# Prompt retention with masked scores of all chunks at once instead of a state carried from chunk to chunk

## The chip, the cores and the metric

One core of one Trainium2 chip. The metric is the device time of one execution in microseconds, the median of several runs; lower is better. All data are fp32; the large projections are computed with operands split into a high and a low part.

## What is computed

The program is one inference step of a decoder with two layers: layer 0 is differential attention, layer 1 multi-scale retention. Both serve a prompt of 512 tokens and eight samples of 8 tokens. The change concerns the retention of the prompt, for each of 8 heads with 256 key and 512 value dimensions. The reference, cut to it:

```python
RET_CHUNK = 128
def retention_chunk(s_prev, q, k, v, log_g):
    c = q.shape[2]
    idx = jnp.arange(c, dtype=jnp.float32)
    diff = idx[:, None] - idx[None, :]
    decay = jnp.where(diff >= 0, jnp.exp(log_g[:, None, None] * jnp.maximum(diff, 0.0)), 0.0)
    scores = jnp.einsum('bhid,bhjd->bhij', q, k) * decay
    o = (jnp.einsum('bhij,bhje->bhie', scores, v)
         + jnp.einsum('bhid,bhde->bhie', q, s_prev) * jnp.exp(log_g[:, None] * (idx + 1.0))[:, :, None])
    k_dec = k * jnp.exp(log_g[:, None] * (c - 1.0 - idx))[:, :, None]
    s_new = jnp.exp(log_g * c)[:, None, None] * s_prev + jnp.einsum('bhjd,bhje->bhde', k_dec, v)
    return s_new, o
```

`retention_prompt` scans this over the four chunks of the prompt from a state of zeros. The outputs `o` are normalised per head, multiplied by the silu of the gate and go through the output projection; the last state is an output too.

## The kernel before, in words

The order of the work is written out by hand as one list of stages, which every engine walks for its own part; semaphores between them carry counts. In layer one a head takes 192 slots. Each slot holds one projection tile (L923): six matmuls of 288 moving columns (high x high, high x low, low x high, each on two halves of the 576 tokens). Eight tiles use one chunk of weights: ScalarE copies it to WH (L1170), VectorE forms the rest WL (L1438), and the first tile of the next chunk waits for it; the tiles of slots that are multiples of 8 open a chunk. Two banks of PSUM are switched every four tiles; at the end of each 32 tiles ScalarE evacuates them (L1186, slots 156 and 159, 188 and 191 among others), and PE needs them free at the next multiple of 32. Between the tiles `retention_work` (L427) puts the retention of the head whose projection is under way:

- slot 100: load of the head's table `hc` (L881), 389 columns of masks and decays, on SyncE's queue; then loads of the sample states and of weights on the same queue
- slot 136: `rs_keys` (PE L1047, ScalarE L1309, VectorE L1634), scores and keys of the samples; VectorE also forms the decayed queries `qd` (L1638) and `qz`
- slot 138: `pad_rows` (L1314), ScalarE issues eight small DMAs that spread the samples' rows, once the keys are copied
- slots 139 + 12c: `ret_scores` (PE L1058): two matmuls of 128 columns (keys of chunk c against queries of chunk c) into bank 4, and two transposes of the keys into bank 5. VectorE masks bank 4 into `sT` (L1664, L1667), ScalarE copies bank 5, scaled, into `kd` (L1324)
- slots 144 + 12c: `ret_out` (L1069): one matmul `sT` x values, and for c > 0 two more, decayed queries x state, 512 columns each, into bank 6; ScalarE copies and squares the result (L1328)
- slots 146 + 12c: `ret_state` (L1079): two matmuls `kd` x values, 512 columns, into banks 4 and 5; VectorE takes them over into the state `Sp` (L1669; a copy for c = 0, L1676 with the decay for c > 0)
- slot 152: `rs_mask` (L1653) for the samples; slot 187: store of the state; slots 190 to 226: norm, gate and store; from 228: the samples' outputs and states, which reach into the slots of the next head.

Each PE stage waits for the banks it writes to be drained (`free`). In the trace all matmuls carry the line of the helper `mm` (L918), all transposes that of `tr` (L921), the copies of ScalarE L1160. An fp32 matmul has two records.

Of the kernel before, what the change touches and what calls it, by code (L numbers as in the profile page):

```python
# [24 lines left out]
MASKED = -1e30  # L25
HC = 128 + 128 + 64 + 64 + 2 + 1 + 2
KRING, VRING = 4, 8
# [7 lines left out]
def shape_tables():  # L35
# [28 lines left out]
    for h in range(HEADS):  # L64
        lg = math.log1p(-2.0 ** (-5 - h))
        w = 1.0 / 16
        diff = i[None] - i[:, None]
        dec = np.where(diff >= 0, np.exp(lg * np.maximum(diff, 0)), 0) * w
        t = row % NQ
        ds = t[None] - t[:, None]  # L70
        decs = np.where((ds >= 0) & (row[None] // NQ == row[:, None] // NQ), np.exp(lg * np.maximum(ds, 0)), 0) * w
        pad = lambda a: np.concatenate([a, np.zeros((128 - a.shape[0], a.shape[1]))])
        spread = lambda a: np.broadcast_to(a[None], (128, a.size))
        r = np.arange(128)
        kz = np.where((r % 32 < 2 * NQ)[:, None] & ((r % 32 // NQ)[:, None] == np.arange(2)[None]),
                      np.exp(lg * (NQ - 1.0 - r % NQ))[:, None], 0) * w
        heads.append(np.concatenate([dec, spread(np.exp(lg * (i + 1))), spread(np.exp(lg * (t + 1.0))), pad(decs), pad(kz),
                                     (np.exp(lg * (127.0 - i)) * w)[:, None],
                                     spread(np.exp(lg * np.array([128.0, 8.0])))], 1))
    eye = np.concatenate([np.eye(128), np.ones((128, 128))], 1)  # L80
# [346 lines left out]
def retention_work(h):  # L427
# [3 lines left out]
    def put(t, *s):  # L431
        at.setdefault(t, []).extend(s)
# [12 lines left out]
    for c in range(4):  # L445
        put(139 + 12 * c, Stage("ret_scores", c=c))
        put(144 + 12 * c, Stage("ret_out", c=c))
        put(146 + 12 * c, Stage("ret_state", c=c))
    put(187, Stage("store_state_p"))
# [181 lines left out]
def hybrid_step_kernel(nc, x_prompt, x_sample, cache_k, cache_v, page_table, state_ret, norm_pre_attn, w_in_attn,  # L631
# [30 lines left out]
    with ctx:  # L662
# [58 lines left out]
        rvT, rqT, rkT = lay("rvT", [128, 2, T]), lay("rqT", [128, 2, T]), lay("rkT", [128, 2, T])  # L721
        qd, kd, Sp = lay("qd", [128, 2, SEQ]), lay("kd", [128, 256]), lay("Sp", [128, 2, 512])
        assert used[0] == KT * T
        hc, rvn, rsg, oN = lay("hc", [128, HC]), lay("rvn", [128, 5, 512]), lay("rsg", [128, 4, T]), lay("oN", [128, 5, 512])
        Sin, sT = lay("Sin", [128, NB, 1024]), lay("sT", [128, 128])
        sTz, qz = lay("sTz", [SMP, 128]), lay("qz", [128, 2, 2, 128])
# [182 lines left out]
        def _(pe):  # L909
# [148 lines left out]
            def ret_scores(g, c_):  # L1058
                lo = c_ * 128
                free(4)  # L1060
                for e in range(2):
                    last = mm(bank[4][:, 0:128], rkT[:, e, lo:lo + 128], rqT[:, e, lo:lo + 128], start=e == 0, stop=e == 1)
                last.then_inc(sem["full4"], 1)
                free(5)
                for e in range(2):
                    last = tr(bank[5][:, e * 128:(e + 1) * 128], rkT[:, e, lo:lo + 128])
                last.then_inc(sem["full5"], 1)

            def ret_out(g, c_):  # L1069
                for n in ("drained4", "drained5", "qd_ready", "drained7"):  # L1070
                    pe.wait_ge(sem[n], c.before(n))
                free(6)
                last = mm(bank[6][:, :], sT[:], rvn[:, c_, :], start=True, stop=c_ == 0)
                if c_:
                    for e in range(2):
                        last = mm(bank[6][:, :], qd[:, e, c_ * 128:c_ * 128 + 128], Sp[:, e, :], start=False, stop=e == 1)
                last.then_inc(sem["full6"], 1)

            def ret_state(g, c_):  # L1079
                free(4)  # L1080
                free(5)
                for e in range(2):
                    mm(bank[4 + e][:, :], kd[:, e * 128:(e + 1) * 128], rvn[:, c_, :]).then_inc(sem[f"full{4 + e}"], 1)

# [49 lines left out]
            def x_tr(g, t, in_low, after, freed):  # L1134
# [7 lines left out]
                for b in range(4):  # L1142
                    for j in range(4):
# [6 lines left out]
                                  rs_keys=rs_keys, ret_scores=lambda g, c: ret_scores(g, c), ret_out=lambda g, c: ret_out(g, c),  # L1150
                                  ret_state=lambda g, c: ret_state(g, c),
                                  rs_state=rs_state, rs_out=rs_out, gate=gate, y_rstd=y_rstd, y_tr=y_tr, x_tr=x_tr))
# [3 lines left out]
        def _(act):  # L1156
# [167 lines left out]
            def ret_scores(g, c_):  # L1324
                act.wait_ge(sem["full5"], c.done("full5"))
                copy(kd[:], bank[5][:, 0:256], scale=hc[:, 386:387]).then_inc(sem["drained5"], 1)

# [79 lines left out]
        def _(dve):  # L1407
# [226 lines left out]
            def rs_keys(g):  # L1634
                dve.wait_ge(sem["head_in"], c.before("head_in"))
                for n in ("full6", "rotated"):
                    dve.wait_ge(sem[n], c.before(n))
                o.link(v.tensor_tensor(qd[:].rearrange("p e (c i) -> p e c i", c=4), rqT[:, :, 0:SEQ].rearrange("p e (c i) -> p e c i", c=4),  # L1638
                                       hc[:, 128:256].rearrange("p (e c i) -> p e c i", e=1, c=1).broadcast_to([128, 2, 4, 128]), MUL))
                for b_ in range(2):  # L1640
                    mine = lambda a: a.rearrange("p e (j b i) -> p e j b i", b=2, i=NQ)[:, :, :, b_, :]
                    ins = v.tensor_tensor(qz[:, b_, :, :].rearrange("p e (j r) -> p e j r", r=32)[:, :, :, b_ * NQ:(b_ + 1) * NQ],
                                          mine(rqT[:, :, SEQ:T]),
                                          mine(hc[:, 256:320].rearrange("p (e n) -> p e n", e=1)).broadcast_to([128, 2, 4, NQ]), MUL)
                    if b_:
                        ins.then_inc(sem["qd_ready"], 1)
                    else:
                        o.link(ins)
                dve.wait_ge(sem["full4"], c.done("full4"))
                v.tensor_tensor(sTz[:].rearrange("p (j r) -> p j r", r=32)[:, :, 0:16], bank[4][0:SMP, 0:SMP].rearrange("p (j r) -> p j r", r=16),  # L1650
                                hc[0:SMP, 320:384].rearrange("p (j r) -> p j r", r=16), MUL).then_inc(sem["drained4"], 1)

            def rs_mask(g):  # L1653
# [3 lines left out]
                for b_ in range(2):  # L1657
                    ins = v.tensor_scalar(kz[:, b_, :], knz[:], hc[:, 384 + b_:385 + b_], None, MUL)
                    if b_:
                        ins.then_inc(sem["kz_ready"], 1)  # L1660
                    else:
                        o.link(ins)

            def ret_scores(g, c_):  # L1664
                dve.wait_ge(sem["full6"], c.before("full6"))
                dve.wait_ge(sem["full4"], c.done("full4"))
                v.tensor_tensor(sT[:], bank[4][:, 0:128], hc[:, 0:128], MUL).then_inc(sem["drained4"], 1)  # L1667

            def ret_state(g, c_):  # L1669
                dve.wait_ge(sem["full6"], c.before("full6"))  # L1670
                dve.wait_ge(sem["sp_out"], c.before("sp_out"))
                for e in range(2):
                    dve.wait_ge(sem[f"drained{4 + e}"], c.before(f"drained{4 + e}"))
                    dve.wait_ge(sem[f"full{4 + e}"], c.done(f"full{4 + e}"))
                    if c_:
                        ins = v.scalar_tensor_tensor(out=Sp[:, e, :], in0=Sp[:, e, :], scalar=hc[:, 387:388], in1=bank[4 + e][:, :],  # L1676
                                                     op0=MUL, op1=ADD)
                    else:
                        ins = v.tensor_copy(Sp[:, e, :], bank[4 + e][:, :])
                    ins.then_inc(sem[f"drained{4 + e}"], 1)  # L1680

# [8 lines left out]
            def rs_state(g, g_, e):  # L1690
                dve.wait_ge(sem["full6"], c.before("full6"))
                for j in range(4):
                    dve.wait_ge(sem[f"full{4 + j}"], c.done(f"full{4 + j}"))
                    mine = Sin[:, 2 * j + g_, e * 512:(e + 1) * 512]
                    v.scalar_tensor_tensor(out=mine, in0=mine, scalar=hc[:, 388:389], in1=bank[4 + j][:, :], op0=MUL, op1=ADD  # L1695
                                           ).then_inc(sem[f"drained{4 + j}"], 1)
# [58 lines left out]
            def x_tr(g, t, in_low, after, freed):  # L1755
                R, src = TILES[t][1], (high, low)[in_low]
                for b in range(4):
# [9 lines left out]
                                sample_gate=sample_gate, carry=carry, rope=rope_, load_rope=load_rope,  # L1767
                                ret_scores=lambda g, c: ret_scores(g, c), ret_state=lambda g, c: ret_state(g, c),
                                ret_norm=ret_norm, ret_rstd=ret_rstd, rs_keys=rs_keys, rs_mask=rs_mask, rs_state=rs_state, gate=gate))


# [72 lines left out]
```

## Time and profile before

| what | value |
|---|---|
| median of 3 runs | 3944.06 us (3943.42 to 3957.97) |
| the profiled execution: its time | 3945.5 us |
| its span, first to last instruction | 3943.7 us |
| mean granted TensorE clock | 0.985 of full |
| the eight heads' retention | from about 2050 to 3460 us of the span |

The page's busy time counts each engine by itself; the list of waits gives, for one engine, how long it sat idle and what released it. A timeline row is one group of equal instructions in a row: start, length, engine, line, operation, output from inputs, number of records, and in brackets the idle time before it. The end of a matmul is modelled and holds the drain of the array, so rows of PE overlap.

### The profile page before, as it was taken

The page shows a single profiled execution, that of the slowest core. Times are in us where ns is not written, and L with a number is a line of the kernel's source. Part 1 is how long each engine was busy: PE and PEld are TensorE (multiplying, and loading weights), DVE is VectorE, ACT ScalarE, POOL GpSimd, SP SyncE. Part 2 cuts the span into 40 slices and gives each one's busy share as a digit, 9 for nine tenths or more (in the row PEclk, how much of TensorE's full clock was granted, in tenths as well). Part 3 has the DMA queues.
Part 4 walks back from the last instruction along what each step waited for, and adds up shares of the span by engine and source line. Part 5 has one row for each costly group of instructions (what it writes and reads, how often), then busy time and mean ns, then how long its engine had stood idle before and what let it go on. Part 6 is the DMA issues. An engine that isn't in the chain of part 4 may idle for free.

```text
span 3943.7 us, 70016 instructions
## 1 busy us (share of the span) xinstructions
PE 3741.5 (95%) x27060; PEld 3298.5 (84%) x27060; DVE 1438.5 (36%) x2197; ACT 1101.9 (28%) x1776; POOL 149.3 (4%) x75
## 2 busy tenths in 40 slices
PE   7999999999999997999899999999999999989998
PEld 6987787778777876777898888988898988879998
DVE  3243334433443344334623333333242424233344
ACT  4233233323332333221422222222222222222221
POOL 1000000200020002002200000000000000000000
PEclk9999999999999998999999999999999999989999
DMA  4455777777767776764332424242434343343332
GB/s 146 143 178 178 235 231 233 209 236 231 236 205 236 231 235 188 234 201 167 122 119 84 161 82 154 82 156 89 151 103 133 109 133 120 121 141 120 105 123 97
DMA packets 470428, 636.62 MB, mean 161 GB/s; under 512 B 39569, under 2 KB 293138, under 8 KB 466962
## 3 DMA queue, kind: packets, MB, share of 16 engines
q1 hardware_dynamic: 405762, 559.90, 45.8%
q10 hardware_dynamic: 64336, 72.24, 5.3%
q8 instruction: 217, 3.56, 0.4%
q14 instruction: 113, 0.93, 0.1%
HBM read 559.80 MB, written 70.65 MB: 160 GB/s over the span
## 4 chain that ended last, share of the span: by engine, by line
PE 80%; DVE 4%; ACT 2%; DMA 2%; issue 2%; ACTq 2%; SPq 1%; POOL 1%; DVEq 0%
PE low_banks L918 58%; PE high_banks L918 15%; PE high_banks L921 8%; DVE WL L1440 1%; DMA area<-in_cache_k 1%; ACT WH L1160 1%; DVE area L1695 1%; ACTq L1352 1%; POOL area L1782 1%; SPq L853 1%; ACTq L1321 1%; ACTq L1322 1%; DMA area<-in_cache_v 0%; ACT area L1160 0%; SPq L854 0%
## 5 line engine op out<-in xcount | busy, mean ns | idle before, releaser
L918 PE MATMUL low_banks<-XH,WH 128*128 128x288 f32 x6656 | 1521.7, 309 | 52.2 <-DVE WL L1440 23.4
L918 PE MATMUL low_banks<-XH,WL 128*128 128x288 f32 x6656 | 1443.4, 297 | 0.0
L918 PE MATMUL low_banks<-XL,WH 128*128 128x288 f32 x6656 | 1441.6, 297 | 0.0
L918 PEld LDWEIGHTS low_banks<-XH,WH 128*128 128x128 f32 x6656 | 1078.0, 191 | 146.8 <-issue 95.8
L918 PEld LDWEIGHTS low_banks<-XL,WH 128*128 128x128 f32 x6656 | 1083.9, 190 | 0.0
L918 PEld LDWEIGHTS low_banks<-XH,WL 128*128 128x128 f32 x6656 | 1082.1, 190 | 0.0
L1440 DVE TENSOR_TENSOR WL<-WR,WH 128x1024 fp32r<-128x1024 f32 x424 | 518.9, 1224 | 902.0 <-ACT WH L1160 896.2
L1160 ACT ACTIVATE WH<-WR 128x1024 fp32r<-128x1024 f32 x424 | 448.6, 1058 | 973.1 <-PE low_banks L918 660.1
L918 PE MATMUL high_banks<-area 128*32 128x512 f32 (+6 forms) x3760 | 658.8, 543 | 51.1 <-DVE area L1667 13.0
L1160 ACT ACTIVATE area<-high_banks 128x512 f32<-128x512 f32 x480 | 270.6, 568 | 1187.4 <-PE high_banks L921 833.2
L921 PEld LDWEIGHTS high_banks<-eye_sb,area 128*128 128x128 f32 (+2 forms) x3032 | 347.9, 142 | 199.6 <-issue 132.5
L921 PE MATMUL high_banks<-eye_sb,area 128*128 128x128 f32 (+2 forms) x3032 | 433.8, 279 | 79.2 <-DVE area L1752 19.5
L918 PEld LDWEIGHTS high_banks<-area 128*32 128x32 f32 (+2 forms) x3760 | 249.1, 148 | 277.1 <-issue 217.2
L1523 DVE COPY area<-high_banks 128x512 f32<-128x512 f32 x256 | 177.1, 692 | 544.1 <-PE high_banks L921 480.9
L1782 POOL TENSOR_TENSOR area<-area,power 128x1 f32<-128x1 f32 (+3 forms) x66 | 124.7, 1890 | 3768.5 <-DVE area L1412 3292.2
L1219 ACT ACTIVATE area<-low_banks 128x288 f32<-128x288 f32 x192 | 78.8, 411 | 355.9 <-PE low_banks L918 339.5
L1695 DVE SCALAR_TENSOR_TENSOR area<-area,high_banks 128x512 f32<-128x512 f32 x128 | 87.2, 745 | 50.6 <-PE high_banks L918 50.4
L1676 DVE SCALAR_TENSOR_TENSOR area<-area,high_banks 128x512 f32<-128x512 f32 x48 | 35.9, 747 | 165.8 <-PE high_banks L918 163.8
L1458 DVE TENSOR_TENSOR area<-low_banks,area 128x288 f32<-128x288 f32 x80 | 36.6, 458 | 140.0 <-PE low_banks L918 139.7
L1220 ACT ACTIVATE area<-low_banks 128x288 f32<-128x288 f32 x192 | 79.0, 411 | 6.1
L1708 DVE TENSOR_TENSOR area<-high_banks,area 128x512 f32<-128x512 f32 (+1 forms) x40 | 25.6, 641 | 113.6 <-PE high_banks L921 113.6
L1445 DVE TENSOR_TENSOR XL<-XL,XH 128x576 fp32r<-128x576 f32 (+1 forms) x48 | 36.1, 752 | 45.4 <-ACT XH L1160 44.1
(106 smaller groups left out, 910.7 us busy)
## 6 DMA issues: line engine op xcount, KB each, us to landing
area<-in_cache_k SPq DMA_DIRECT2D x512, 256.0 KB, 4.1
area<-in_cache_v SPq DMA_DIRECT2D x512, 256.0 KB, 3.9
WR<-in_w_in_ret SPq DMA_DIRECT2D x196, 512.0 KB, 3.6
WR<-in_w_in_attn SPq DMA_DIRECT2D x132, 512.0 KB, 5.4
out<-area ACTq DMA_DIRECT2D x73, 512.0 KB, 4.5
area<-in_state_ret SPq DMA_DIRECT2D x64, 512.0 KB, 5.6
WR<-in_w_out_ret SPq DMA_DIRECT2D x64, 512.0 KB, 3.3
WR<-in_w_out_attn SPq DMA_DIRECT2D x32, 512.0 KB, 5.4
```

The source lines that it names most:

```text
L853: page = sp.value_load(pt[0:1, b * PAGES + p:b * PAGES + p + 1], min_val=0, max_val=src.shape[0] - 1)
L918: return nc.tensor.matmul(out, a, b, start=start, stop=stop, skip_group_check=True)
L921: return nc.tensor.matmul(out, a, ident[0:n, 0:n], start=True, stop=True, is_transpose=True, skip_group_check=True)
L1160: return nc.scalar.activation(out, in_, ACT.Copy, scale=scale)
L1219: o.link(nc.scalar.activation(dst[:, 0:HALF], bank[2 * cb][:, 0:HALF], f))
L1220: last = nc.scalar.activation(dst[:, HALF:T], bank[2 * cb + 1][:, 0:HALF], f)
L1321: act.dma_start(knz[padded, :], kn_s[rows, :]).then_inc(sem["padded_in"], 16)
L1322: act.dma_start(rvz[padded, :], rvn[rows, 4, :]).then_inc(sem["padded_in"], 16)
L1440: v.tensor_tensor(WL[:, slot, :, :], WR[:, slot, :, :], WH[:, slot, :, :].bitcast(f32), SUB).then_inc(sem["w_lo"], 1)
L1523: v.tensor_copy(KTs[u % 2][:, :, pp * 128:(pp + 1) * 128], bank[5][:, :].rearrange("p (j s) -> p j s", j=4)).then_inc(sem["drained5"], 1)
L1695: v.scalar_tensor_tensor(out=mine, in0=mine, scalar=hc[:, 388:389], in1=bank[4 + j][:, :], op0=MUL, op1=ADD).then_inc(sem[f"drained{4 + j} ...
L1782: nc.gpsimd.tensor_tensor(out, a, power[0:R, 0:n], ALU.pow).then_inc(sem[name], 1)
```

## The change

The state isn't carried between chunks. Chunk c's keys are multiplied with the queries of chunks c to 3 (512 - 128c columns), masked with a decay table of 512 columns and kept in four buffers; the output of chunk c is the sum over k = 0 .. c of scores times values, in PSUM. The decayed keys of all four chunks are kept, scaled with one column each for the distance to the end of the prompt, and the state is formed once, by four accumulated matmuls for each half. The decayed queries go. The stages move: `ret_scores` to 139 + 5c, `ret_out` to 148 + 8c, `ret_state` to 177, once. The table has 647 columns.

```diff
-HC = 128 + 128 + 64 + 64 + 2 + 1 + 2
+DEC_S, MASK_S, ROWS_S, DEC_K, DEC_8, HC = 512, 576, 640, 642, 646, 647
...
-        diff = i[None] - i[:, None]
+        diff = np.arange(512.0)[None] - i[:, None]
...
     for c in range(4):
-        put(139 + 12 * c, Stage("ret_scores", c=c))
-        put(144 + 12 * c, Stage("ret_out", c=c))
-        put(146 + 12 * c, Stage("ret_state", c=c))
+        put(139 + 5 * c, Stage("ret_scores", c=c))
+        put(148 + 8 * c, Stage("ret_out", c=c))
+    put(177, Stage("ret_state"))
...
-        qd, kd, Sp = lay("qd", [128, 2, SEQ]), lay("kd", [128, 256]), lay("Sp", [128, 2, 512])
+        kd, Sp = lay("kd", [128, 4, 256]), lay("Sp", [128, 2, 512])
...
-        Sin, sT = lay("Sin", [128, NB, 1024]), lay("sT", [128, 128])
+        Sin = lay("Sin", [128, NB, 1024])
+        sT = [lay(f"sT{c}", [128, SEQ - 128 * c]) for c in range(4)]
...
                 for e in range(2):
-                    last = mm(bank[4][:, 0:128], rkT[:, e, lo:lo + 128], rqT[:, e, lo:lo + 128], start=e == 0, stop=e == 1)
+                    last = mm(bank[4][:, 0:SEQ - lo], rkT[:, e, lo:lo + 128], rqT[:, e, lo:SEQ], start=e == 0, stop=e == 1)
...
             def ret_out(g, c_):
-                for n in ("drained4", "drained5", "qd_ready", "drained7"):
+                for n in ("drained4", "drained7"):
                     pe.wait_ge(sem[n], c.before(n))
                 free(6)
-                last = mm(bank[6][:, :], sT[:], rvn[:, c_, :], start=True, stop=c_ == 0)
-                if c_:
-                    for e in range(2):
-                        last = mm(bank[6][:, :], qd[:, e, c_ * 128:c_ * 128 + 128], Sp[:, e, :], start=False, stop=e == 1)
+                for k in range(c_ + 1):
+                    last = mm(bank[6][:, :], sT[k][:, (c_ - k) * 128:(c_ - k + 1) * 128], rvn[:, k, :], start=k == 0, stop=k == c_)
...
-            def ret_state(g, c_):
+            def ret_state(g):
                 free(4)
                 free(5)
                 for e in range(2):
-                    mm(bank[4 + e][:, :], kd[:, e * 128:(e + 1) * 128], rvn[:, c_, :]).then_inc(sem[f"full{4 + e}"], 1)
+                    for k in range(4):
+                        last = mm(bank[4 + e][:, :], kd[:, k, e * 128:(e + 1) * 128], rvn[:, k, :], start=k == 0, stop=k == 3)
+                    last.then_inc(sem[f"full{4 + e}"], 1)
...
-                copy(kd[:], bank[5][:, 0:256], scale=hc[:, 386:387]).then_inc(sem["drained5"], 1)
+                copy(kd[:, c_, :], bank[5][:, 0:256], scale=hc[:, DEC_K + c_:DEC_K + c_ + 1]).then_inc(sem["drained5"], 1)
...
-                o.link(v.tensor_tensor(qd[:].rearrange("p e (c i) -> p e c i", c=4), rqT[:, :, 0:SEQ].rearrange("p e (c i) -> p e c i", c=4),
-                                       hc[:, 128:256].rearrange("p (e c i) -> p e c i", e=1, c=1).broadcast_to([128, 2, 4, 128]), MUL))
...
                 dve.wait_ge(sem["full4"], c.done("full4"))
-                v.tensor_tensor(sT[:], bank[4][:, 0:128], hc[:, 0:128], MUL).then_inc(sem["drained4"], 1)
-
-            def ret_state(g, c_):
-                dve.wait_ge(sem["full6"], c.before("full6"))
+                n = SEQ - 128 * c_
+                v.tensor_tensor(sT[c_][:], bank[4][:, 0:n], hc[:, 0:n], MUL).then_inc(sem["drained4"], 1)
+
+            def ret_state(g):
                 dve.wait_ge(sem["sp_out"], c.before("sp_out"))
                 for e in range(2):
-                    dve.wait_ge(sem[f"drained{4 + e}"], c.before(f"drained{4 + e}"))
                     dve.wait_ge(sem[f"full{4 + e}"], c.done(f"full{4 + e}"))
-                    if c_:
-                        ins = v.scalar_tensor_tensor(out=Sp[:, e, :], in0=Sp[:, e, :], scalar=hc[:, 387:388], in1=bank[4 + e][:, :],
-                                                     op0=MUL, op1=ADD)
-                    else:
-                        ins = v.tensor_copy(Sp[:, e, :], bank[4 + e][:, :])
-                    ins.then_inc(sem[f"drained{4 + e}"], 1)
+                    v.tensor_copy(Sp[:, e, :], bank[4 + e][:, :]).then_inc(sem[f"drained{4 + e}"], 1)
```

## Rows read from the trace of the kernel before

**Rows 1.** The page, busy time of PE: share of the span, instructions.
```profile
PE 3741.5 (95%) x27060; PEld 3298.5 (84%) x27060; DVE 1438.5 (36%) x2197; ACT 1101.9 (28%) x1776; POOL 149.3 (4%) x75
```

**Rows 2.** PE's waits from 2050 to 3460 us: releaser, total, times, longest (all of them).
```profile
PE low_banks L918 <- DVE WL L1440: 13.7, 7, 2.0
PE high_banks L918 <- DVE area L1667: 13.0, 8, 2.2
```

**Rows 3.** Timeline of PE in head 1, the retention of the prompt.
```profile
2246.08 0.61 PE L918 MATMUL high_banks<-area 128*128 128x128 f32 x4
...
2252.14 1.13 PE L918 MATMUL high_banks<-area 128*128 128x512 f32 x2 [1.25 <-DVE area L1667]
...
2260.39 0.61 PE L918 MATMUL high_banks<-area 128*128 128x128 f32 x4
...
2265.04 2.74 PE L918 MATMUL high_banks<-area 128*128 128x512 f32 x6
...
2269.21 1.88 PE L918 MATMUL high_banks<-area 128*128 128x512 f32 x4
...
2274.92 0.61 PE L918 MATMUL high_banks<-area 128*128 128x128 f32 x4
```

**Rows 4.** Timeline of ACT and its queue in head 1.
```profile
2243.90 0.38 ACT L1160 ACTIVATE area<-high_banks 64x256 f32<-64x256 f32 x1 [1.92 <-PE high_banks L921]
2244.31 0.54 ACTq L1321 DMA_DIRECT2D area<-area  x1
...
2248.72 0.61 ACTq L1322 DMA_DIRECT2D area<-area  x1
2249.44 1.06 ACT L1160 ACTIVATE WH<-WR 128x1024 fp32r<-128x1024 f32 x1 [5.16 <-issue]
...
2267.86 0.60 ACT L1160 ACTIVATE area<-high_banks 128x512 f32<-128x512 f32 x1 [4.70 <-PE high_banks L918]
...
2269.26 0.41 ACT L1219 ACTIVATE area<-low_banks 128x288 f32<-128x288 f32 x1
```

**Rows 5.** Timeline of DVE in head 1.
```profile
2250.53 1.23 DVE L1440 TENSOR_TENSOR WL<-WR,WH 128x1024 fp32r<-128x1024 f32 x1 [6.75 <-ACT WH L1160]
2251.79 0.29 DVE L1667 TENSOR_TENSOR area<-high_banks,area 128x128 f32<-128x128 f32 x1
```

**Rows 6.** DVE's groups by shape, 2050 to 3460 us: count, busy us, mean ns, idle before.
```profile
L1676 DVE SCALAR_TENSOR_TENSOR area<-area,high_banks 128x512 f32<-128x512 f32 x48 | 35.9, 747 | 165.8 <-PE high_banks L918 163.8
L1708 DVE TENSOR_TENSOR area<-high_banks,area 128x512 f32<-128x512 f32 x28 | 19.4, 695 | 69.2 <-PE high_banks L921 69.2
...
L1667 DVE TENSOR_TENSOR area<-high_banks,area 128x128 f32<-128x128 f32 x32 | 9.4, 293 | 42.4 <-PE high_banks L918 41.8
```

**Rows 7.** Timeline of PE around the same wait in heads 0, 2, 4 and 6.
```profile
2060.49 1.84 PE L918 MATMUL high_banks<-area 128*128 128x512 f32 x2 [2.09 <-DVE area L1667]
...
2070.35 0.61 PE L918 MATMUL high_banks<-area 128*128 128x128 f32 x4
...
2443.13 2.07 PE L918 MATMUL high_banks<-area 128*128 128x512 f32 x2 [2.19 <-DVE area L1667]
...
2828.17 1.13 PE L918 MATMUL high_banks<-area 128*128 128x512 f32 x2 [1.50 <-DVE area L1667]
...
3210.61 1.66 PE L918 MATMUL high_banks<-area 128*128 128x512 f32 x2 [2.05 <-DVE area L1667]
```

**Rows 8.** Stretches with PE alone: us, busy (records), granted clock, DMA share, GB/s.
```profile
2060.80:2064.10 3.30, 3.30 (x11) 0.50 0.49 159
...
2443.10:2446.40 3.30, 3.27 (x8) 0.50 0.52 159
...
3211.10:3214.40 3.30, 3.30 (x12) 0.50 0.51 159
...
2826.00:2833.00 7.00, 5.50 (x29) 1.00 0.26 80
```

**Rows 9.** The page's DMA issues: count, KB each, us from issue to landing.
```profile
area<-ret_heads SPq DMA_DIRECT2D x8, 194.5 KB, 3.5
```

More of the change, by code:

```diff
@@ L76, in shape_tables @@
                       np.exp(lg * (NQ - 1.0 - r % NQ))[:, None], 0) * w
-        heads.append(np.concatenate([dec, spread(np.exp(lg * (i + 1))), spread(np.exp(lg * (t + 1.0))), pad(decs), pad(kz),
-                                     (np.exp(lg * (127.0 - i)) * w)[:, None],
-                                     spread(np.exp(lg * np.array([128.0, 8.0])))], 1))
+        heads.append(np.concatenate([dec, spread(np.exp(lg * (t + 1.0))), pad(decs), pad(kz),
+                                     np.exp(lg * (511.0 - i[:, None] - 128 * np.arange(4)[None])) * w,
+                                     spread(np.exp(lg * np.array([8.0])))], 1))
     eye = np.concatenate([np.eye(128), np.ones((128, 128))], 1)
@@ L721, in hybrid_step_kernel @@
         rvT, rqT, rkT = lay("rvT", [128, 2, T]), lay("rqT", [128, 2, T]), lay("rkT", [128, 2, T])
-        qd, kd, Sp = lay("qd", [128, 2, SEQ]), lay("kd", [128, 256]), lay("Sp", [128, 2, 512])
-        assert used[0] == KT * T
+        kd, Sp = lay("kd", [128, 4, 256]), lay("Sp", [128, 2, 512])
+        assert used[0] <= KT * T
+        used[0] = KT * T
         hc, rvn, rsg, oN = lay("hc", [128, HC]), lay("rvn", [128, 5, 512]), lay("rsg", [128, 4, T]), lay("oN", [128, 5, 512])
-        Sin, sT = lay("Sin", [128, NB, 1024]), lay("sT", [128, 128])
+        Sin = lay("Sin", [128, NB, 1024])
+        sT = [lay(f"sT{c}", [128, SEQ - 128 * c]) for c in range(4)]
         sTz, qz = lay("sTz", [SMP, 128]), lay("qz", [128, 2, 2, 128])
@@ L1150, in _ @@
                                   rs_keys=rs_keys, ret_scores=lambda g, c: ret_scores(g, c), ret_out=lambda g, c: ret_out(g, c),
-                                  ret_state=lambda g, c: ret_state(g, c),
+                                  ret_state=ret_state,
                                   rs_state=rs_state, rs_out=rs_out, gate=gate, y_rstd=y_rstd, y_tr=y_tr, x_tr=x_tr))
@@ L1643, in rs_keys @@
                                           mine(rqT[:, :, SEQ:T]),
-                                          mine(hc[:, 256:320].rearrange("p (e n) -> p e n", e=1)).broadcast_to([128, 2, 4, NQ]), MUL)
+                                          mine(hc[:, DEC_S:DEC_S + SMP].rearrange("p (e n) -> p e n", e=1)).broadcast_to([128, 2, 4, NQ]), MUL)
                     if b_:
@@ L1650, in rs_keys @@
                 v.tensor_tensor(sTz[:].rearrange("p (j r) -> p j r", r=32)[:, :, 0:16], bank[4][0:SMP, 0:SMP].rearrange("p (j r) -> p j r", r=16),
-                                hc[0:SMP, 320:384].rearrange("p (j r) -> p j r", r=16), MUL).then_inc(sem["drained4"], 1)
+                                hc[0:SMP, MASK_S:MASK_S + SMP].rearrange("p (j r) -> p j r", r=16), MUL).then_inc(sem["drained4"], 1)
             def rs_mask(g):
@@ L1657, in rs_mask @@
                 for b_ in range(2):
-                    ins = v.tensor_scalar(kz[:, b_, :], knz[:], hc[:, 384 + b_:385 + b_], None, MUL)
+                    ins = v.tensor_scalar(kz[:, b_, :], knz[:], hc[:, ROWS_S + b_:ROWS_S + b_ + 1], None, MUL)
                     if b_:
@@ L1694, in rs_state @@
                     mine = Sin[:, 2 * j + g_, e * 512:(e + 1) * 512]
-                    v.scalar_tensor_tensor(out=mine, in0=mine, scalar=hc[:, 388:389], in1=bank[4 + j][:, :], op0=MUL, op1=ADD
+                    v.scalar_tensor_tensor(out=mine, in0=mine, scalar=hc[:, DEC_8:DEC_8 + 1], in1=bank[4 + j][:, :], op0=MUL, op1=ADD
                                            ).then_inc(sem[f"drained{4 + j}"], 1)
@@ L1767, in _ @@
                                 sample_gate=sample_gate, carry=carry, rope=rope_, load_rope=load_rope,
-                                ret_scores=lambda g, c: ret_scores(g, c), ret_state=lambda g, c: ret_state(g, c),
+                                ret_scores=lambda g, c: ret_scores(g, c), ret_state=ret_state,
                                 ret_norm=ret_norm, ret_rstd=ret_rstd, rs_keys=rs_keys, rs_mask=rs_mask, rs_state=rs_state, gate=gate))
```

## The prediction, made before the changed kernel was run

> **What bounds the kernel now.** I read the page's busy line first: TensorE (PE) is busy 3741.5 us of a span of 3943.7 [rows 1]. Its work is therefore the time, and only two things can shorten the kernel: less PE work, or less idle time of PE. VectorE at 36% and ScalarE at 28% cost something only where PE waits for them, so instructions saved there are worth nothing by themselves.
>
> Next comes the list of PE's waits in the stretch of layer one that holds the eight heads [rows 2]. It has two entries alone: 13.0 us in 8 waits for L1667, the VectorE mask of the scores, and 13.7 us in 7 waits for the low half of a weight chunk (WL). There is no wait for L1676, the update of the running state. The chain from chunk to chunk that the change does away with costs PE nothing today.
>
> The timeline of PE in head 1 says the same [rows 3]. From the second score block at 2260.39 to the third at 2274.92 lie 14.53 us. They hold 12 projection tiles, one score block (about 0.6) and five matmuls of 512 columns. One of these is 2.74 - 1.88 = 0.86 us (six records against four, two records to a matmul), so 4.3 in all, and 9.6 us stay for 12 tiles, 0.80 each. The sum closes with no gap. The only gap of this stretch is the 1.25 us ahead of 2252.14, the first output matmul of the head, at slot 144.
>
> Where does that gap come from? On ScalarE [rows 4] the copy at 2243.90 is followed by eight DMA issues for the padded rows, from 2244.31 to 2249.33. Only behind them runs the split of the weights into WH (2249.44, 1.06 us). VectorE takes its turn for WL at 2250.53 and for the first mask at 2251.79 [rows 5]. PE starts at 2252.14, 0.06 us behind the mask's end. This chain starts from rs_keys (slot 136), ahead of the first score block: it doesn't know how long that block is. This is what the forecast hangs on.
>
> **The change, part by part.** *PE, scores.* Chunk c's score matmuls get 512 - 128c moving columns in place of 128, two matmuls each. Extra columns in a head: 2 x (384 + 256 + 128) = 1536. Price: two matmuls of 512 columns show 1.88 us, two of 128 show 0.61 [rows 3]; the drain at the end is the same in both, so 1.27 us for 768 columns, 1.65 ns a column. That is 2.54 us a head, **+20.3 us** for eight. No engine hides it, since PE itself is the bound.
>
> *PE, outputs and state.* Before: 1 + 3 + 3 + 3 = 10 matmuls of 512 columns for the outputs; after: 1 + 2 + 3 + 4 = 10. State: 4 x 2 before, 2 x 4 after. Transposes of the keys: 8 and 8. All of this at **0**. Accumulating in PSUM moves the additions from VectorE into matmuls that were there already.
>
> *VectorE.* It loses the decayed queries (L1638) and six state updates of 0.747 us a head, two copies out of PSUM stay; its masks grow from 4 x 0.293 to something between 0.293 and 0.695 each (L1708 is the same kind of operation on 128x512 out of PSUM) [rows 6]. PE doesn't wait for these operations but at the first mask, so they count 0 on the path, and that one mask counts +0.40 us. ScalarE keeps all its copies, with another scale column: 0.
>
> *The wait at slot 144.* The first output matmul moves to slot 148, and the second score block comes to slot 144 in its place. It needs bank 4 free, hence the same first mask. So the wait changes its owner, and isn't removed by the move. But in head 1 PE would come to slot 144 1.27 us later, at 2250.89 + 1.27 = 2252.16; the mask would end at 2251.79 + 0.695 = 2252.49, and with 0.06 us for the release PE goes on at 2252.55, after 0.39 us. Over the heads the mean wait is 13.0 / 8 = 1.63; new 1.63 - 1.27 + 0.40 = 0.76, in sum 6.1, so **-6.9 us**. Bounds: all of it gone (-13.0), or nothing absorbed and the mask longer (+3.2).
>
> *The clock.* After three of the eight waits, those of 2.09, 2.19 and 2.05 us, PE's granted clock was 0.50 (1.2 GHz) for a stretch; after the wait of 1.50 it stayed at 1.00, 2.4 GHz [rows 7, 8]. Price: from the first output matmul to the second score block head 0 took 2070.35 - 2060.49 = 9.86 us, head 1 2260.39 - 2252.14 = 8.25 for the same work [rows 3, 7], so 1.61 us for a fall. The longest of these waits would shrink to 2.19 - 0.87 = 1.32, below the 1.50 that did no harm. I take all three falls as gone: **-4.8 us**. Bounds: none gone (0), or a fall in all eight heads (+8.1).
>
> Here the Trainium skill speaks otherwise: its page "TensorE: Matmul & The Clock Gate", section "HAM oscillation — how this bites in real kernels", counts only idle gaps longer than any of these as a cause of a throttled clock. By it the three falls would have another cause and would stay, and the sum would lack the 4.8 us. The trace has the fall right behind each of the three longest waits, so my sum goes by the rows.
>
> *What else moves.* The second to fourth score blocks each wait for the mask before them; they stand 5 tiles (4 us) apart, and the masks take 0.7 at most. At slot 156 the output block is followed by the evacuation of the projection's banks, which PE needs at slot 160. ScalarE takes 2269.26 - 2267.86 = 1.40 us for its two passes over the output [rows 4] and 0.82 for the evacuation's two copies of 0.41. Today 1.7 us of state matmuls stand in between as well; afterwards only 4 tiles, 3.2 us, cover 0.06 + 1.40 + 0.82 = 2.3. It holds with 0.9 us over: 0. The state's 8 matmuls become one block of 6.9 us at slot 177; VectorE then splits the next WL behind its two copies, and PE wants that only 7 tiles (5.6 us) after the block: 0. The head table grows from 389 to 647 columns, so its load from 194.5 KB to 323.5; it takes 3.5 us now [rows 9] and is issued at slot 100 for use at 136, 29 us later: 0 even at twice the time. The 13.7 us of waits for WL come from slots that the change doesn't touch, behind DMA issues for the sample states: 0, with some luck in whether a clock fall follows them.
>
> **Sum:** +20.3 - 6.9 - 4.8 = +8.6 us. Against the profiled execution's own span that is 3943.7 + 8.6 = 3952.3. Its time was 3945.5, which is 1.8 above the span and 1.4 above the median of the three runs (3944.06). Carried to the median: 3952.7.
>
> **The rivals.** (1) *The clock's falls stay.* They follow from something else than the waits' length, or the shorter waits do it too. For it: the waits for WL, of up to 2.0 us [rows 2], are followed by a fall in three of seven cases by my count, so the length alone does not decide. Sum +20.3 - 6.9 = +13.4, so 3957.5. The skill's rule ends here too.
>
> (2) *The wait isn't absorbed; slower.* Place: slot 144. If ScalarE's DMA issues and its split of WH come later by what PE loses in the longer block, PE waits the full 1.63 and the longer mask: 16.2 us in all, +3.2, with a mean of 2.03 us. That is the length at which the clock fell [rows 7, 8], so it would fall in all eight heads, five more: +8.1. Sum 20.3 + 3.2 + 8.1 = +31.6, so 3975.7. It decides, with the falls as they are today, from the point where less than 3.8 of the 16.2 us is absorbed (20.3 + 3.2 - 3.8 = 19.7); with more falls earlier. Against it: the chain starts from a copy ahead of the score block [rows 4]; for it: the wait was 1.25 us in one head and 2.19 in another, so this chain is not a fixed one [rows 3, 7].
>
> (3) *More comes back.* The emptier VectorE and the longer block leave no wait at slot 144 (-13.0), no fall there (-4.8), and the falls behind the WL waits, I count three, don't come by luck (-4.8): 20.3 - 22.6 = -2.3, so 3941.8.
>
> (4) *Faster by more than can be told.* All waits and falls of these heads together, 13.0 + 13.7 + 4.8 + 4.8 = 36.3, against 20.3 would give -16.0, 3928.1. Even this isn't outside the 0.5%, so only something that no row shows could do it.
>
> **How the numbers follow.** A measurement of this kernel can tell about 0.5% from no change, 19.7 us. Forecast 0.54; rival (1) 0.22; rival (2) 0.10; rival (3) 0.12; rival (4) 0.02. The forecast, (1) and (3) lie within 0.5%: same 0.88; slower 0.10 from (2), faster 0.02 from (4). The range takes in (3) at its low end and (1) with a few falls of the clock on top, each 1.6 us: 3941 to 3963. Left out are (2), (4) and a little at both ends.
>
> **What would show it.** In the profile after: PE's busy time up by some 20 us; two score matmuls of 512 columns at 1.88 us; no state updates (L1676) on VectorE any more; in the list of PE's waits the mask stays the releaser, now of a score block, with about 6 us in 8 waits of at most 1.4; the same 13.7 us for WL; the clock at 1.00 behind every score block. A mask wait of over 1.5 us, or one at a place other than slot 144, would make me wrong, and a total beyond 3963.8 us would mean that the longer blocks opened a wait which I have costed at nothing.

## The result and the profile after

The changed kernel takes **3960.26 us** (median of 19 runs, 3956.92 to 3967.49), the kernel before 3945.91 (19 runs, 3937.18 to 3957.97) measured along with it. The ratio is 1.0039, 95% interval 1.0033 to 1.0045. That is slower by 0.4%, some 14 to 15 us, and inside the 0.5% that the prediction called "same". The forecast was +8.6. The direction holds; some 40% of the size is missing from the forecast and has to be found. Two runs taken later, one of the changed kernel at 5893.86 us (mean granted clock 0.582) and one of the kernel before at 5256.97 (0.652), ran at a far lower clock and are left out of the ratios and medians below.

The profiled execution took 3957.83 us, with a span of 3956.0. Its busy line, which answers to [rows 1]:

```profile
PE 3757.1 (95%) x27060; PEld 3302.8 (83%) x27060; DVE 1398.8 (35%) x2141; ACT 1102.2 (28%) x1776; POOL 149.4 (4%) x75
```

VectorE lost 39.7 us of work and 56 instructions, ScalarE nothing, and PE gained 15.6 us of busy time with the same number of records where the prediction named some 20 (busy time falls where the clock is higher, and this profile has three falls of the clock fewer in the retention, so this isn't the price of the columns by itself). Line numbers have moved by one or two: mm is L920, tr L923, ScalarE's copies L1162, the mask L1668, WL L1442.

PE's waits between 2050 and 3475 us, all of them, against [rows 2] (who waited, releaser, total, times, longest):

```profile
PE low_banks L920 <- DVE WL L1442: 13.7, 7, 2.0
PE high_banks L920 <- DVE area L1668: 4.6, 8, 1.1
PE low_banks L920 <- ACT area L1222: 0.6, 1, 0.6
```

The 13.0 us behind the first mask have become 4.6. The waits for WL are the same to a tenth. A third entry is new, of one wait.

Timeline of PE in head 1, against [rows 3]:

```profile
2250.05 1.88 PE L920 MATMUL high_banks<-area 128*128 128x512 f32 x4
...
2256.51 1.56 PE L920 MATMUL high_banks<-area 128*128 128x384 f32 x4 [0.36 <-DVE area L1668]
...
2262.96 1.03 PE L920 MATMUL high_banks<-area 128*128 128x256 f32 x4
...
2268.04 0.61 PE L920 MATMUL high_banks<-area 128*128 128x128 f32 x4
...
2278.38 2.74 PE L920 MATMUL high_banks<-area 128*128 128x512 f32 x6
...
2287.35 3.60 PE L920 MATMUL high_banks<-area 128*128 128x512 f32 x8
...
2294.77 7.04 PE L920 MATMUL high_banks<-area 128*128 128x512 f32 x16
```

The score blocks shrink from 1.88 to 0.61 us, the output blocks grow by one matmul each, and the state is one block of eight matmuls. The wait stands ahead of the second score block, at slot 144, with 0.36 us where the prediction worked out 0.39 for this very head.

Timeline of DVE in head 1, against [rows 5]:

```profile
2254.50 1.22 DVE L1442 TENSOR_TENSOR WL<-WR,WH 128x1024 fp32r<-128x1024 f32 x1 [6.76 <-ACT WH L1162]
2255.76 0.69 DVE L1668 TENSOR_TENSOR area<-high_banks,area 128x512 f32<-128x512 f32 x1
```

Behind the late WL comes the wide mask with 0.69 us. So far the profile agrees with the steps. What remains is the clock. Stretches of PE (us, busy and records, granted clock, DMA share, GB/s): three behind waits for WL and one behind the wait at slot 144.

```profile
2206.10:2209.40 3.30, 3.30 (x16) 0.50 0.88 273
2591.90:2595.20 3.30, 3.30 (x16) 0.50 0.93 304
2977.60:2980.90 3.30, 3.30 (x16) 0.50 0.89 286
...
2256.00:2262.00 6.00, 5.64 (x35) 1.00 0.28 90
```

Behind none of the eight waits for the mask does the clock fall to 1.2 GHz any more. It falls behind three of the seven waits for WL, in every second head. In the kernel before it was three falls behind the mask and three behind WL.

### The profile page after: what moved, and what is told of

Same layout as the page of the kernel before. It is cut to its first block and busy times, and to the rows that moved or that the text cites. A ratio compares the mean times of both kernels' runs of the same rounds, so it can differ in the third digit from the quotient of the medians.

```text
span 3956.0 us, 69816 instructions
## 1 busy us (share of the span) xinstructions
PE 3757.1 (95%) x27060; PEld 3302.8 (83%) x27060; DVE 1398.8 (35%) x2141; ACT 1102.2 (28%) x1776; POOL 149.4 (4%) x75
## 5 line engine op out<-in xcount | busy, mean ns | idle before, releaser
L920 PE MATMUL low_banks<-XH,WH 128*128 128x288 f32 x6656 | 1510.3, 307 | 53.8 <-DVE WL L1442 22.3
L920 PE MATMUL low_banks<-XH,WL 128*128 128x288 f32 x6656 | 1444.3, 297 | 0.0
L920 PE MATMUL low_banks<-XL,WH 128*128 128x288 f32 x6656 | 1442.8, 297 | 0.0
L920 PEld LDWEIGHTS low_banks<-XH,WH 128*128 128x128 f32 x6656 | 1077.1, 191 | 135.6 <-issue 85.3
L920 PEld LDWEIGHTS low_banks<-XH,WL 128*128 128x128 f32 x6656 | 1083.8, 190 | 0.0
L920 PEld LDWEIGHTS low_banks<-XL,WH 128*128 128x128 f32 x6656 | 1082.7, 190 | 0.0
L1442 DVE TENSOR_TENSOR WL<-WR,WH 128x1024 fp32r<-128x1024 f32 x424 | 519.0, 1224 | 1002.0 <-ACT WH L1162 996.3
L1162 ACT ACTIVATE WH<-WR 128x1024 fp32r<-128x1024 f32 x424 | 448.5, 1058 | 1065.1 <-PE low_banks L920 752.0
L920 PE MATMUL high_banks<-area 128*32 128x512 f32 (+6 forms) x3760 | 672.6, 548 | 43.5 <-DVE area L1525 11.3
L1162 ACT ACTIVATE area<-high_banks 128x512 f32<-128x512 f32 x480 | 270.6, 569 | 1160.2 <-PE high_banks L923 837.4
L923 PEld LDWEIGHTS high_banks<-eye_sb,area 128*128 128x128 f32 (+2 forms) x3032 | 346.9, 142 | 208.6 <-issue 139.0
L923 PE MATMUL high_banks<-eye_sb,area 128*128 128x128 f32 (+2 forms) x3032 | 431.6, 278 | 81.7 <-DVE area L1746 19.8
L920 PEld LDWEIGHTS high_banks<-area 128*32 128x32 f32 (+2 forms) x3760 | 253.2, 147 | 287.4 <-issue 233.0
L1525 DVE COPY area<-high_banks 128x512 f32<-128x512 f32 x256 | 177.0, 692 | 546.9 <-PE high_banks L923 483.9
L1689 DVE SCALAR_TENSOR_TENSOR area<-area,high_banks 128x512 f32<-128x512 f32 x128 | 87.2, 744 | 51.2 <-PE high_banks L920 51.2
L1222 ACT ACTIVATE area<-low_banks 128x288 f32<-128x288 f32 x192 | 79.1, 412 | 6.0
L1674 DVE COPY area<-high_banks 128x512 f32<-128x512 f32 x16 | 11.1, 692 | 115.0 <-PE high_banks L920 115.0
```

Of the source, the lines that this page charges most:

```text
L920: return nc.tensor.matmul(out, a, b, start=start, stop=stop, skip_group_check=True)
L923: return nc.tensor.matmul(out, a, ident[0:n, 0:n], start=True, stop=True, is_transpose=True, skip_group_check=True)
L1162: return nc.scalar.activation(out, in_, ACT.Copy, scale=scale)
L1222: last = nc.scalar.activation(dst[:, HALF:T], bank[2 * cb + 1][:, 0:HALF], f)
L1442: v.tensor_tensor(WL[:, slot, :, :], WR[:, slot, :, :], WH[:, slot, :, :].bitcast(f32), SUB).then_inc(sem["w_lo"], 1)
L1525: v.tensor_copy(KTs[u % 2][:, :, pp * 128:(pp + 1) * 128], bank[5][:, :].rearrange("p (j s) -> p j s", j=4)).then_inc(sem["drained5"], 1)
```

## The experiments

Ratios are to the kernel before, measured along with each run.

**1. Wide scores alone, in the kernel before.** The extra columns are computed and not read.

```diff
-                    last = mm(bank[4][:, 0:128], rkT[:, e, lo:lo + 128], rqT[:, e, lo:lo + 128], start=e == 0, stop=e == 1)
+                    last = mm(bank[4][:, 0:SEQ - lo], rkT[:, e, lo:lo + 128], rqT[:, e, lo:SEQ], start=e == 0, stop=e == 1)
```

> The kernel before, with its schedule and its running state, but the score matmuls as wide as in the change (512, 384, 256, 128 columns); the extra columns are computed and not read. Theory A (the added columns cost their 1.65 us per 1000, and only the wait behind the first mask gives something back, because its releaser does not depend on PE): PE's busy time +20 us, the wait for L1667 falls from 13.0 us to 1.63 - 1.27 = 0.36 us in the mean, about 3 to 4 in sum, so about +10 us without falls of the clock, +5 to +8 with those that the long waits had caused. Rival B (the releaser moves along with PE, nothing absorbed): the wait stays at 13 and the time grows by 20 us.

Measured: 3949.58 us (12 runs), ratio to before 1.0013 (1.0002 to 1.0024), about +5 to +7. PE's waits in the retention:

```profile
PE low_banks L918 <- DVE WL L1440: 13.7, 7, 2.0
PE high_banks L918 <- DVE area L1667: 2.5, 5, 0.8
```

Theory A holds and B falls: the releaser stays where it was and PE comes later. 10.5 us of waiting are swallowed by the wider blocks. But this kernel has all the columns of the change and is some 10 us faster than it. So not all of the change's loss is in the scores.

**2. The changed kernel, a second and a third time.** Unchanged.

> The changed kernel once more, to see which part of its time repeats. Theory A: the waits for the mask and for WL come out as in the first profile (about 4.6 and 13.7 us); the falls of the clock do not stand behind the mask waits, and those behind the WL waits (three of seven in the first profile) are drawn anew. Rival C (the clock falls as often as before, at other places): as many falls between 2050 and 3475 us as in the kernel before, six.

> The changed kernel a third time. Layer 0, which the change doesn't touch, ended 4 us later in the four profiles with the parallel form (its head 0 reaches rs_keys at 2052.5 to 2056.3) than in the six with the running state (2047.8 to 2053.0), and PE's waits there for loads of cached keys were 12.4 to 15.4 us against 8.5 to 12.1. If this belongs to the changed program, head 0 starts at 2054 or later again with 12 us or more of these waits; if it is chance, it lies anywhere between 2048 and 2056. In the retention the waits for the mask (4.6) and for WL (13.7) stay as they were.

Measured: 3962.85 and 3959.87 us (ratios 1.0044 and 1.0039). The mask's waits were 4.9 and 4.5 us in 8, those for WL 13.7 in 7 both times. The clock fell behind four and three of the waits for WL and behind none of the mask's: with the first profile 3, 4, 3 falls in the retention. That isn't as often as the six of the first profile before (rival C), and it doesn't look drawn by lot either: heads 0, 2, 4 in all three profiles, and head 6 once. The third profile also came to head 0 at 2050.9 us with 15.2 us of waits for cached keys, which neither branch of its expectation had together; more on that below.

**3. The kernel before, once more.** Unchanged.

> The kernel before once more. If the clock's fall behind a wait of about 2 us is a matter of chance, the three mask waits of 2.05 to 2.19 us won't all be followed by one again, and the forecast's 4.8 us for the clock was too much: over executions it would be nearer to 1.5 falls, 2.4 us. If it is fixed by the length, all waits over 2.0 us have a fall behind them again.

Measured: 3943.9 us, one run; four falls in the retention in place of six. Timeline of PE and the stretches behind:

```profile
2058.65 1.63 PE L918 MATMUL high_banks<-area 128*128 128x512 f32 x2 [2.12 <-DVE area L1667]
...
2440.83 1.13 PE L918 MATMUL high_banks<-area 128*128 128x512 f32 x2 [1.74 <-DVE area L1667]
...
2963.17 0.53 PE L918 MATMUL low_banks<-XH,WH 128*128 128x288 f32 x2 [1.96 <-DVE WL L1440]
...
3205.27 1.38 PE L918 MATMUL high_banks<-area 128*128 128x512 f32 x2 [1.82 <-DVE area L1667]
```

```profile
2059.20:2062.50 3.30, 3.30 (x13) 0.50 0.51 159
2581.50:2584.80 3.30, 3.30 (x16) 0.50 0.82 255
2963.80:2967.10 3.30, 3.30 (x16) 0.50 0.85 255
3206.10:3209.40 3.30, 3.30 (x14) 0.50 0.48 152
```

The clock fell behind the mask waits of 2.12 and 1.82 us, and not behind that of 1.74; of seven waits for WL, all of 1.94 to 1.96 us, it fell behind two (2581.15 and 2963.17). So length plays a part, since no shorter wait of the retention was followed by a fall, and it doesn't decide alone, since waits for WL of the same length at the same place went either way. That the moment at which a wait comes is the other part is my inference; no run here varied it by itself. Neither of the two expectations was quite it. The Trainium skill's rule that the prediction cites (page "TensorE: Matmul & The Clock Gate", section "HAM oscillation — how this bites in real kernels") asks for idle gaps longer than these. The trace doesn't agree: here the clock fell behind a gap of 1.82 us.

**4. A wider table alone, in the kernel before.** While looking for the missing time I saw PE's waits for cached keys in layer 0, which the change doesn't touch: in the changed kernel 13.7 us, in the kernel before 9.8.

```diff
-HC = 128 + 128 + 64 + 64 + 2 + 1 + 2
+HC = 128 + 128 + 64 + 64 + 2 + 1 + 2 + 258
...
-                                     spread(np.exp(lg * np.array([128.0, 8.0])))], 1))
+                                     spread(np.exp(lg * np.array([128.0, 8.0]))), np.zeros((128, 258))], 1))
```

> The kernel before with a head table of 647 columns in place of 389, the further ones zeros that nothing reads (the table lies in device memory and is loaded to the chip for each head, as in the change). PE's waits for the loads of cached keys in layer 0, which the change doesn't touch, were 9.8, 10.1 and 8.5 us in three profiles of kernels with the small table and 13.7, 14.8 and 15.4 in three with the large one. Theory E (the larger constant shifts what lies behind it, or otherwise disturbs these loads): these waits are 13 to 16 us here and the time is 4 to 6 us above before. Rival F (it goes with something else in the change, or is chance): 8 to 10 us and no difference in time.

Measured: 3945.6 us (11 runs), ratio 1.0007 (0.9998 to 1.0016); the waits for cached keys 9.4 us. Theory E falls. As the prediction costed it at 0, the larger load shows no price beyond the noise. Its profile is also a third one of the schedule before: 12.2 us behind the mask, four falls in the retention.

**5. The DMA issues of the padded rows two slots later, in the changed kernel and in the kernel before.**

```diff
-    put(138, Stage("pad_rows"))
+    put(140, Stage("pad_rows"))
```

> The changed kernel with the eight DMA issues for the padded samples' rows (pad_rows) moved from slot 138 to slot 140, behind the split of the next weights and the first copy of the keys on ScalarE. Theory A (the mask's wait at slot 144 comes from these issues): the wait for the mask is gone, 4.6 us less, nothing else changes; time 3956. Rival D (the masks are too wide for their slots): the wait stays at about 0.6 us a head.

> The kernel before, running state and all, with pad_rows moved from slot 138 to 140. Theory A: the waits behind the first mask (13.0 us) are gone, with the falls of the clock that followed them: 13 to 18 us faster than before, 3926 to 3931. Rival D (the wait moves to the copy of the keys or to the weights): no more than 4 us faster.

Measured, changed kernel: 3947.3 us (11 runs), ratio to before 1.0010. ScalarE in head 1 of it, and the stretch of the whole retention on PE:

```profile
2249.07 0.38 ACT L1162 ACTIVATE area<-high_banks 64x256 f32<-64x256 f32 x1 [1.92 <-PE high_banks L923]
2249.35 1.05 ACT L1162 ACTIVATE WH<-WR 128x1024 fp32r<-128x1024 f32 x1
2253.45 0.48 ACT L1162 ACTIVATE area<-high_banks,area 128x256 f32<-128x256 f32 x1 [3.04 <-PE high_banks L923]
2253.95 0.54 ACTq L1323 DMA_DIRECT2D area<-area  x1
```

```profile
2050.00:3450.00 1400.00, 1385.76 (x9636) 1.00 0.37 120
```

WH is now split at once, and the issues wait behind it; compare [rows 4]. The waits for the mask are gone. The gain is 13 us, though, where 3956 was expected: the clock didn't fall once in the retention of this profile, although the waits for WL were still there (13.7 us in 7). Heads now followed each other every 191.15 us, and the waits came at moments that cost nothing. With the 4.6 us of waits, the three falls fewer explain some 5 us more; what is left of the difference I can't assign from one profile, and the pattern of the falls is seen in this one profile alone.

Kernel before: 3928.05 us (5 runs), ratio 0.9959 (0.9946 to 0.9973), and its list of waits for the retention holds only WL, 13.7 us in 7. Inside the expected range; rival D is out. The mask never was too slow: ScalarE's issues held it up.

**6. The stores of the sample states one slot later: alone in the kernel before, and with 5 in both.**

```diff
-        put(262 + 12 * g, *[Stage("store_state", b=2 * j + g) for j in range(4)])
+        put(263 + 12 * g, *[Stage("store_state", b=2 * j + g) for j in range(4)])
```

> The kernel before with the stores of the sample states one slot later and nothing else. Theory G: the 13.7 us of waits for WL gone and the falls behind them (two to three of 1.6 us), the 13 us behind the first mask unchanged: 3926 to 3931, about as much as pad_rows alone gave (3928). If the two moves share a cause, less.

> The changed kernel with pad_rows at slot 140 and the stores of the sample states moved one slot later (262 + 12g to 263 + 12g), so that ScalarE's split of the next weights goes ahead of four DMA issues. Theory G (the waits for WL, 1.95 us in 7 heads, come from these issues, and falls of the clock follow some of them): the 13.7 us of waits for WL between 2050 and 3475 us are gone, and no fall of the clock stands in this stretch; 14 to 18 us below the changed kernel with pad_rows moved alone (3947), so 3930. Rival H: the waits stay, since VectorE's state updates and not the issues delay the split.

> The kernel before with both moves. Theory A and G together: all 26.7 us of waits and the falls behind them gone, 3946 - 27 - 5 to 10 = 3909 to 3914. Against the changed kernel with both moves this is the price of the parallel form when neither has a wait: theory A says 20 us (the 12288 added columns at 1.65 ns), less if the longer score blocks still cover something.

> The kernel before with both moves, a second time: 3908.9 us again, within 4 us; heads of 186.31 us; no fall of the clock in the retention.

Measured: alone 3928.02 us (ratio 0.9954, 0.9941 to 0.9966), with no wait for WL in the retention and 13.0 us behind the mask. Both moves in the changed kernel: 3933.82 (0.9973, 0.9964 to 0.9982). Both moves in the kernel before: **3908.89 and 3907.43** (0.9911, 0.9895 to 0.9927, and 0.9907, 0.9893 to 0.9922), the fastest of all. Theory G holds, H falls. The lists of PE's waits for the retention are empty but for one entry of the changed kernel, the same 0.6 us for L1222 as above. Moving the stores gave the changed kernel 13.5 us, a little under the 14 to 18 expected: that is the 13.7 us of waits alone, since in experiment 5 no fall of the clock was left behind them. ScalarE in head 0 of the kernel before and, behind it, with both moves:

```profile
2197.91 2.02 ACTq L1352 DMA_DIRECT2D out<-area  x2
2200.02 2.15 ACT L1160 ACTIVATE WH<-WR 128x1024 fp32r<-128x1024 f32 x2 [10.62 <-issue]
...
2189.26 1.06 ACT L1160 ACTIVATE WH<-WR 128x1024 fp32r<-128x1024 f32 x1 [3.84 <-PE low_banks L918]
2193.16 3.29 ACTq L1352 DMA_DIRECT2D out<-area  x4
2196.90 1.06 ACT L1160 ACTIVATE WH<-WR 128x1024 fp32r<-128x1024 f32 x1 [6.58 <-PE low_banks L918]
```

Before, two splits of WH stand one behind the other, both behind the stores. With the stores one slot later the first split goes ahead of them.

Against each other, in one session, the two kernels with both moves differ by 24.9 us, where theory A said 20. The retention's part of that is in experiment 7; the rest is taken up under layer 0 below. The clock, PE alone, both moves in the kernel before:

```profile
2060.00:3420.00 1360.00, 1358.62 (x9605) 1.00 0.38 123
```

**7. The price of the columns, without any wait.** Both moves in the kernel before, and the wide scores of experiment 1.

> The running state with both moves, no waits left, and the score matmuls widened to 512, 384, 256 and 128 columns, the extra columns not read. A head takes 186.31 us without them and 189.02 in the parallel form. Theory A (the columns are the whole price): 186.31 + 2.54 = 188.85 us or a little more a head, the time 20 to 22 us above the 3908.9 of the kernel with both moves. Rival I (the price is in the accumulating matmuls of the outputs and the state): less than 187.5 us a head.

Measured: 3927.5 us (5 runs), 20.1 above the kernel with both moves run beside it. Two heads in a row, by the start of rs_keys on PE (64 columns): the running state with both moves, the same with wide scores, and the parallel form with both moves.

```profile
2423.54 0.45 PE L918 MATMUL high_banks<-area 128*64 128x64 f32 x4
...
2609.85 0.45 PE L918 MATMUL high_banks<-area 128*64 128x64 f32 x4
```

```profile
2424.05 0.45 PE L918 MATMUL high_banks<-area 128*64 128x64 f32 x4
...
2612.93 0.45 PE L918 MATMUL high_banks<-area 128*64 128x64 f32 x4
```

```profile
2432.89 0.45 PE L920 MATMUL high_banks<-area 128*64 128x64 f32 x4
...
2621.91 0.45 PE L920 MATMUL high_banks<-area 128*64 128x64 f32 x4
```

186.31, 188.88 and 189.02 us a head. The columns cost 2.57 us a head, where the prediction had 2.54 from its rows; everything else in the parallel form costs 0.14. Rival I falls: within a head it is the columns. The whole kernels tell a little more: the parallel form with both moves takes 3933.82 us and this one 3927.5, and only some 2 of these 6 us lie in the heads (8 x 0.14, and the 0.6 us of L1222).

## Why the prediction was right, and what it missed

**The score columns.** Predicted +20.3, measured 8 x 2.57 = 20.6. Pricing a matmul by the difference of two rows with the same drain was exact to 2%.

**Outputs and state at 0.** Nearly: 8 x 0.14 = 1.1 us. No VectorE instruction saved was worth anything, as costed: 39.7 us less work there, and no wait of PE is seen to have gone away for it.

**The wait at slot 144.** Predicted -6.9 (13.0 to 6.1). In three profiles of each schedule (before, experiments 3 and 4; the changed kernel three times) it went from 13.0, 12.5 and 12.2 to 4.6, 4.9 and 4.5: -7.9. The mechanism is shown by experiments 1 and 5: a releaser that is tied to ScalarE's DMA issues, ahead of the block that became longer, so PE arrives later and waits less. Rival (2), the slower one, is out.

**The slack at slot 160.** Predicted 0.9 us over, so 0. It held in seven heads. In head 0 ScalarE has to load its table for the gate's silu in just this place. Timeline of ACT in head 0 of the changed kernel, and of PE:

```profile
2079.30 0.19 ACT L1332 ACTIVATION_READ_ACCUMULATOR area<-high_banks 128x1 f32 x1
2079.56 1.28 ACT L1221 ACT_TABLE_LOAD   x1
```

```profile
2081.85 0.50 PE L920 MATMUL low_banks<-XH,WH 128*128 128x288 f32 x2 [0.58 <-ACT area L1222]
```

The same load stands there in the kernel before, where no wait followed. 1.28 us more in the chain made a wait of 0.58, so the slack is 0.7. The step had the right size and overlooked one instruction: +0.6 us.

**The clock: this step was mis-sized.** "I take all three falls as gone: -4.8 us." The falls behind the mask did go, in all three profiles of the changed kernel; in three of the schedule before they were 3, 2 and 3. But the falls behind the waits for WL, which I costed at 0 "with some luck", went from 3, 2 and 1 to 3, 4 and 3. In the mean 4.7 falls became 3.3, worth 1.3 x 1.61 = 2.2 us and not 4.8. The forecast's profile happened to have more falls than its kernel usually has, and I gave all of them back. The forecast and rival (1), which gives back none (+13.4), each have part of it; rival (1)'s number is the nearer one. Of the two reasons it gave, that the shorter mask waits still bring falls is wrong; that something besides the length decides is borne out, at the waits for WL.

**Layer 0: a term that the sum didn't have.** Five profiles of kernels with the parallel form show 13.7, 14.8, 15.4, 12.4 and 15.2 us of waits for cached keys, nine with the running state 8.2 to 12.4, with a mean of 10.1 against 14.3. Head 0 reaches rs_keys at 2054.0 us in the mean of the five and at 2050.0 in the mean of the nine. One row of PE's waits from 0 to 2044 us, of the changed kernel and of the kernel before:

```profile
PE high_banks L923 <- DMA area<-in_cache_k: 13.7, 10, 4.1
```

```profile
PE high_banks L921 <- DMA area<-in_cache_k: 9.8, 9, 4.2
```

Nothing in the diff is at work there. The size of the table isn't the cause (experiment 4), nor are the wider matmuls by themselves (8.5 and 8.2 us in experiments 1 and 7). What is left is chance over few profiles or something about the whole program, such as where it lies in memory, which was not tried. The runs without a wait in the retention point the same way: the 24.9 us of experiment 6, less 8 x 2.71 and 0.6 in the heads, leave 2.7, and the 6 us of experiment 7, less 2, leave some 4. The third profile of the changed kernel came to head 0 at 2050.9 in spite of 15.2 us of these waits, so even the 4 us are a mean over few profiles. The cause stays open.

**The sum anew:** 20.6 + 1.1 + 0.6 - 7.9 - 2.2 = +12.2 in the retention, and some +4 in layer 0: 16, against 14 to 15 by the runs. The forecast came out inside its range because the range was wide enough for the two terms that it had wrong, the clock and layer 0, both of which made the changed kernel slower; only 1.0 us more absorbed at slot 144 went the other way. The trace pair of the first result alone would have misled: its span difference is 12.3 us, with its own count of falls on either side in it.

## What to carry to other kernels

Where one engine is the bound, count what a restructuring adds on that engine and nothing it takes off the others: here the recurrence that no engine on the critical path waited for cost nothing, and triangular scores over all chunks cost 1536 columns a head more. Look next for who really releases the few waits there are; here two groups of DMA issues on ScalarE, placed one or two slots too early, cost 27 us of waiting, and moving them by one or two slots gave 0.9% where rewriting the algorithm lost 0.4%. When a term rests on events that differ between executions of the same kernel, such as falls of the clock, look at more than one profile before giving it back.

## What the runs showed of the hardware that I had not expected

TensorE's clock fell to 1.2 GHz behind waits as short as 1.81 us (that one in the kernel of experiment 4). In the retention all eleven waits for the mask of 1.81 us or more were followed by a fall, over four profiles, and only 21 of 63 waits for WL of 1.94 to 1.97 us, over nine; none of up to 1.74 us was. That isn't a limit for the whole program: in layer 0 of the changed kernel, between long stretches of matmuls, PE waited 1.71 us up to 365.39, and the granted clock was 0.50 from 366.40 to 369.70.

With waits at fixed places in a loop the falls came in a pattern with the loop's turn: in every second head of the changed kernel, whose heads take 191.8 us without a fall, in three profiles, and behind none of the seven waits where a head takes 191.15 us, in one. So a change that only shifts the length of a turn may win or lose 1.6 us in some of the turns with no wait changed; no run here shifted the length alone.

And a DMA issue for a few rows held ScalarE's queue for 0.61 us, now and then 1.4 to 1.6: eight of them kept it from a split of 1.06 us on which PE depended.
